# Block inverse by 32 changed columns per level, and attention steps with one wait for the scores

## The reference

```
s = einsum('bqkgd,bskd->bkgqs', q, k) * scale
p = softmax(s, axis=-1)
o = einsum('bkgqs,bskd->bqkgd', p, v)
```

```
sa = einsum('bhvk,bhk->bhv', S, kk_t)
S = S * w_t - sa * (kk_t * a_t) + v_t * k_t
y = einsum('bhvk,bhk->bhv', S, r_t)
```

## Time and profile before

| | before |
|---|---|
| median of three runs | 2634.2 us |
| the profiled execution, its own time | 2641.69 us |
| its span, first to last instruction | 2639.9 us |
| TensorE busy | 2530.2 us (96%) |
| VectorE, ScalarE, GpSimd busy | 791.9, 594.8, 234.0 us |
| mean granted TensorE clock | 0.988 |

### The profile page before, as it was taken

One profiled execution on the slowest core, in us unless ns is written; L12 is line 12 of the kernel. 1 busy time (PEld: TensorE's weight loads), 2 busy tenths in 40 slices (PEclk: granted clock), 3 DMA queues, 4 the chain that ended last, 5 costly groups with the idle time before them and its releaser, 6 DMA issues. The chain is left out here.

```text
span 2639.9 us, 51609 instructions
## 1 busy us (share of the span) xinstructions
PE 2530.2 (96%) x23368; PEld 1512.2 (57%) x23368; DVE 791.9 (30%) x1611; ACT 594.8 (23%) x1273; POOL 234.0 (9%) x243
## 2 busy tenths in 40 slices
PE   6999999999999999999999999999999999998998
PEld 4444654455555554444444446466566666687887
DVE  2542333343434422121010002441544444321101
ACT  3353332122223211020000002441332322211100
POOL 0000000122122300000000000000022222100000
PEclk9999999999999999999999999999999999999999
DMA  7102111233232334232222224112121112145553
GB/s 278 51 17 72 49 49 56 88 106 105 67 129 66 129 98 152 80 96 72 80 78 73 80 73 149 46 66 87 56 74 58 50 51 63 54 135 177 153 153 108
DMA packets 64410, 239.14 MB, mean 91 GB/s; under 512 B 7008, under 2 KB 8048, under 8 KB 63424
## 3 DMA queue, kind: packets, MB, share of 16 engines
q1 hardware_dynamic: 61824, 220.23, 26.6%
q0 software_dynamic: 2368, 15.61, 1.6%
HBM read 234.76 MB, written 1.05 MB: 89 GB/s over the span
## 5 line engine op out<-in xcount | busy, mean ns | idle before, releaser
L420 PE MATMUL psum<-normed,panel_ring 128*128 128x512 f32 (+1 forms) x3136 | 1161.2, 515 | 4.5 <-ACT normed L648 3.4
L420 PEld LDWEIGHTS psum<-normed,panel_ring 128*128 128x128 f32 x3136 | 572.6, 190 | 433.6 <-issue 384.2
L420 PE MATMUL psum<-arena 64*64 64x64 f32 (+5 forms) x15256 | 566.5, 244 | 47.1 <-DVE arena L1599 16.4
L420 PE MATMUL psum<-arena,panel_ring 128*128 128x512 f32 (+1 forms) x1792 | 606.6, 492 | 1.8 <-ACT arena L1067 1.8
L420 PEld LDWEIGHTS psum<-arena 64*64 64x64 f32 (+3 forms) x15256 | 379.3, 137 | 329.1 <-issue 215.8
L420 PEld LDWEIGHTS psum<-arena,panel_ring 128*128 128x128 f32 x1792 | 333.7, 190 | 226.3 <-issue 200.7
L714 DVE TENSOR_REDUCE softmax_stats<-psum 128x1 f32<-128x512 f32 (+1 forms) x144 | 83.9, 600 | 170.6 <-PE psum L420 169.4
L739 ACT ACTIVATE arena<-psum,softmax_stats 128x512 f32<-128x512 f32 (+1 forms) x144 | 87.8, 613 | 209.4 <-DVE softmax_stats L714 123.6
L1814 DVE TENSOR_TENSOR arena<-arena 128x512 f32<-128x512 f32 (+1 forms) x64 | 35.7, 559 | 305.1 <-ACT arena L1801 305.1
L1690 DVE SCALAR_TENSOR_TENSOR arena<-psum,modulation,arena 128x256 f32<-128x256 f32 x24 | 10.9, 481 | 313.9 <-PE psum L420 313.9
L1573 POOL TENSOR_SCALAR arena<-arena 128x64 f32<-128x64 f32 x96 | 72.3, 768 | 358.4 <-DVE arena L1612 212.0
(11 more groups left out here) (158 smaller groups left out, 1404.5 us busy)
## 6 DMA issues: line engine op xcount, KB each, us to landing
panel_ring<-panels SPq DMA_DIRECT2D x398, 512.0 KB, 3.6
arena<-panels SPq DMA_DIRECT2D x16, 512.0 KB, 14.8
arena<-small_b POOLq DMA_DIRECT2D x2, 2176.0 KB, 9.3
arena<-bias_d POOLq DMA_DIRECT2D x2, 2048.0 KB, 9.1
arena<-x_t SPq DMA_DIRECT2D x2, 1024.0 KB, 7.5
arena<-x_t POOLq DMA_DIRECT2D x1, 2048.0 KB, 14.1
arena<-const_r POOLq DMA_DIRECT2D x2, 800.0 KB, 6.6
arena<-small_c POOLq DMA_DIRECT2D x2, 768.0 KB, 4.7
```

Source lines behind the costliest of these rows:

```text
L420: return nc.tensor.matmul(out, lhsT, rhs, start=start, stop=stop, skip_group_check=check)
```

## The change

In the levels, only half the columns are computed. At level j the blocks of width w = 2^j alternate: `old` picks the blocks that are only read at this level, `new` those that change. Group T moves 32 columns of the identity (`old`), group B the 32 `new` columns of `X`, group C the 32 columns of `B`; weights stay 64x64, and the number of matmuls stays the same. Their results lie in the first half of a PSUM bank. ScalarE evacuates B with one instruction for both directions (512 elements a partition). VectorE's four instructions have 256 elements a partition, and write into `Xt` and `X` with gaps of w elements between runs of w.

In attention the first score matmul of a step waits for both exponentials of the item before, the second has no wait; and PV is issued ahead of the transposes.

```diff
+                    if exp_done.at(2 * (s - 1) + 2) > 0:
+                        e.wait_ge(exp_done.h, exp_done.at(2 * (s - 1) + 2))
                     for i in range(2):
-                        if exp_done.at(2 * (s - 1) + i + 1) > 0:
-                            e.wait_ge(exp_done.h, exp_done.at(2 * (s - 1) + i + 1))
                         mm(psum[:, i, :nk], q_of(...), k_of(t, i, nk), True, True).then_inc(scores_full.h, 1)
-                if s >= 2 and s - 2 < n_items:      # transposes of item s-2
-                    ...
                 if s >= 3 and (s - 3) % 2 == 1:     # PV
                     ...
+                if s >= 2 and s - 2 < n_items:      # transposes of item s-2, same text
+                    ...
...
-        nt, B, Xt, t2 = chunks(lw), chunks(L), chunks(e2), be
+        nt, B, Xt, t2 = chunks(lw), L, chunks(e2), be
+        half_token = lambda c: slice(c * CHUNK // 2, (c + 1) * CHUNK // 2)
+        blocks = lambda a, j, n: a.rearrange("p (b two w) -> p b two w", two=2, w=1 << j)[:, :, n, :]
+        old = lambda a, d, j: blocks(a, j, d)
+        new = lambda a, d, j: blocks(a, j, 1 - d)
...
-  p = mm(psum[half[hd], tb + d, token(c)], X[tside(d, hd), d, c, :], eye[tside(d, hd)], True, True)
+  p = mm(psum[half[hd], tb + d, half_token(c)], X[tside(d, hd), d, c, :], old(eye[tside(d, hd)], d, j), True, True)
-  p = mm(psum[half[hd], bb + d, token(c)], nt[tside(d, hd), d, c, :], X[tside(d, hd), d, c, :], True, True)
+  p = mm(psum[half[hd], bb + d, half_token(c)], nt[tside(d, hd), d, c, :], new(X[tside(d, hd), d, c, :], d, j), True, True)
-  p = mm(psum[tside(d, hd), tb + d, token(c)], Xt[half[hd], d, c, :], B[half[hd], d, c, :], True, True)
+  p = mm(psum[tside(d, hd), tb + d, half_token(c)], Xt[half[hd], d, c, :], B[half[hd], d, half_token(c)], True, True)
...
-                for d in range(2):
-                    p = nc.scalar.activation(B[:, d], chunked(psum[:, bb + d, :]), ACT.Copy)
-                p.then_inc(b_copied.h, 1)
+                nc.scalar.activation(B[:, :, :T // 2], psum[:, bb:bb + 2, :T // 2], ACT.Copy).then_inc(b_copied.h, 1)
...
-                    p = nc.vector.tensor_copy(Xt[:, d], chunked(psum[:, tb + d, :]))
+                    p = nc.vector.tensor_copy(old(Xt[:, d].rearrange("p c t -> p (c t)"), d, j),
+                                              psum[:, tb + d, :T // 2].rearrange("p (b w) -> p b w", w=1 << j))
...
-                    p = nc.vector.copy_predicated(X[:, d], wide(level(d, j), NCH), chunked(psum[:, tb + d, :]))
+                    w = 1 << j
+                    p = nc.vector.copy_predicated(
+                        X[:, d].rearrange("p c (b two w) -> p c b two w", two=2, w=w)[:, :, :, 1 - d, :],
+                        new(level(d, j), d, j).unsqueeze(1).broadcast_to([P, NCH, CHUNK // (2 * w), w]),
+                        psum[:, tb + d, :T // 2].rearrange("p (c b w) -> p c b w", c=NCH, w=w))
```

More of the change, by code:

```diff
@@ L673, in pe @@
                     t, half, nk = groups[g]
+                    if exp_done.at(2 * (s - 1) + 2) > 0:
+                        e.wait_ge(exp_done.h, exp_done.at(2 * (s - 1) + 2))
                     for i in range(2):
-                        if exp_done.at(2 * (s - 1) + i + 1) > 0:
-                            e.wait_ge(exp_done.h, exp_done.at(2 * (s - 1) + i + 1))
                         mm(psum[:, i, :nk], q_of(t, i, 2 * half + qt), k_of(t, i, nk), True, True).then_inc(scores_full.h, 1)
-                if s >= 2 and s - 2 < n_items:
[L679 to L687, removed]
                 if s >= 3 and (s - 3) % 2 == 1:
@@ L698, in pe @@
                     p.then_inc(pv_done.h, 1)
+                if s >= 2 and s - 2 < n_items:
+                    n = s - 2
+                    nk = groups[items[n][0]][2]
+                    for i in range(2):
+                        e.wait_ge(probs_ready.h, probs_ready.at(2 * n + i + 1))
+                        if probsT_ready.at(2 * (n - 1) + i + 1) > 0:
+                            e.wait_ge(probsT_ready.h, probsT_ready.at(2 * (n - 1) + i + 1))
+                        for kt in range(nk // P):
+                            p = nc.tensor.transpose(psum[:, 2 + i, kt * P:(kt + 1) * P], prob[:, n % 2, i, kt * P:(kt + 1) * P], ident)
+                        p.then_inc(probsT_full.h, 1)
                 yield
```

## The result

The kernel after takes 2621.48 us (median of 8 runs, 2614.57 to 2628.59), the kernel before beside it 2636.09 us (8 runs, 2630.48 to 2641.67). The ratio is 0.9949 with a 95% interval of 0.9931 to 0.9967. A second set, 11 runs against 20, gave 0.9959 (0.9944 to 0.9973). So the change is worth 11 to 13 us where the forecast says 22. The profiled execution took 2628.59 us, its span 2626.8 us, at a mean granted clock of 0.987 (before 0.988). It was the slowest of its eight runs; their mean clock is 0.9895.

The account below looks back on a forecast made before the run. TensorE, busy 96% of the span, was taken as the bound, so only its waits could pay; 0 - 8.1 - 12.5 - 1.4 = -22 us took the median of 2634.2 us to 2612 us, range 2596 to 2629.

Parts of the forecast that it names:

- The matmul groups: Groups T, B and C in the levels: halving moving columns saves 0 us, since the weight load sets the pace.
- Wait C: Levels: TensorE's wait ahead of group C for the copy of B shrinks with shorter evacuations, -8.1 us.
- Wait X: Levels: TensorE's wait for the masked write into X shrinks as that write gets shorter, -12.5 us.
- I take 433: Levels: a masked write of 256 elements was taken to last 433 ns whatever its runs, against 718 for 512.
- Rival (b): Levels: evacuations with gaps don't get shorter, Wait X stays, Wait C shrinks by ScalarE's part; 2625 us, chance 0.09.
- A wait gives back at most its length: Levels: caps each copy-of-B wait's gain at its idle time, counted with 0.07 us more than its row says.
- rival (d): Gain spent elsewhere: attention steps late (+6), longer X waits become VectorE backlog at the next filler; about -6, 2628 us, chance 0.08.
- Rival (c): Levels: with half the columns streaming the clock falls to 1.2 GHz more often; slower, up to 2678 us, chance 0.05.
- The clock is full in all 40 slices: Whole run before the change: the profile's clock row was read as showing full clock throughout.
- in the scan fewer records keep the full clock: Scan after the levels: 429 records in 31 us, under half a level's, keep 2.4 GHz; argued against Rival (c).
- Attention: Attention steps: PV first saves 24 switches, -2.4 us; longer waits at three places cost +1; together -1.4 us.
- waiting together loses nothing: Attention A and D: two heads' scores run side by side, so one wait is free when the second is late anyway.

Follow-up runs that it names:

- dup64: The changed kernel, but each level group moves its 32 columns twice (64 moving), only the first copy evacuated; 0.9945 of the kernel before.
- dup64_levels: dup64 with the attention steps of the kernel before; 0.9952 of the kernel before, 12.6 us faster.
- the three pairs above: Kernels with 32 against 64 moving columns, short evacuations in both, attention alike within a pair; 32 slower by 1 and 4 us, by 5 us, and faster by half a us.
- attention_only: The kernel before with only the change's attention steps, levels as before; 1.8 us faster, with an interval that holds zero.
- cols32_long: The changed kernel's 32-column groups, but evacuations as long as before and the attention of before; 1.0044 of the kernel before.
- cols64_long: cols32_long with each group moving its 32 columns twice, so 64 columns move; 1.0013 of the kernel before.

## Why the prediction came out as it did

- **The matmul groups, 0 us: right.** 1.14 and 2.07 us a burst where "1.1 to 1.16" and 2.1 were to be seen, and dup64 shows no cost for double the columns.
- **Wait C, -8.1 us: right.** 7.4 us by the sum of standstills; the row for the copy of B went from 5.9 to 0.4 us.
- **Wait X, -12.5 us: too large by 2.** 10.5 us. The step that failed is "I take 433": 16 of 80 masked writes, at level 1, took 711 to 772 ns, as long as before (pair 1.28 us). Three waits hang on a level 1; they stood at 0.56, 1.81 and 0.54 us and came to 0.52, 2.11 and 0.50. Rival (b) held there and nowhere else. The row went from 16.4 to 6.0 us, 5 forecast.
- **That what TensorE doesn't wait for is gained: mis-sized by about 6 us.** This step is in the sentence "A wait gives back at most its length", to which no loss was put. Stops inside the groups rose from 9 to 16 us; that they are stops for instruction blocks is my reading. It is the mechanism of rival (d), the gain spent elsewhere, but in a place that (d) doesn't name. With -17.9 + 6.4 = -11.5 us the levels come close to the 12.6 us that dup64_levels measured at an unchanged clock.
- **The clock, 0 us: wrong, by 0 to 5 us.** Rival (c) in a weak form. Falls like that of rows 10 happened for 27 us of the levels' time and not 7 in the profiled run, the slowest of the change; the mean clock was 0.0015 to 0.004 lower than before in the four kernels with 32 columns and short evacuations. Times 1.55 to 2.2 us per 0.001 this would be 2 to 9 us, and the three pairs above show 0 to 5. "The clock is full in all 40 slices" read the digit 9 as full: the trace of before spends 64 us at 1.2 GHz in its mean of 0.988, and has two falls in the levels, from 953.1 and from 2185.3, not one. The argument "in the scan fewer records keep the full clock" held records of other lengths, at PE busy 30.91 of 31.00 us, against those of a level, at 26.56 of 31.00, and so did not bear on a level.
- **Attention, -1.4 us: right in sum, 1.8 measured with a wide interval.** PV first gave 1.5 us in B and D of layer 0. The cost was put in the wrong place. The longer wait of 3.0 us in A did grow, to 3.8 us. But D of layer 1 refutes "waiting together loses nothing": five waits of 3.9 us in all, +1.0 us.
- **The sum.** -22 forecast; by the parts -17.9 + 6.4 - 1.8 + (0 to 5) = -13 to -8; measured -13.4 and -10.8. That the parts meet the measurement is no proof of them: two traces with the levels unchanged (before, attention_only) already differ by 4.7 us in them, so no part is known better than to 2 or 3 us.

## What to carry to other kernels

When TensorE has short, dense work with many instructions, removing its waits may give back less than they last; look at the row "issue" and at stops that recur every 127 matmuls before counting a wait as gained. Halving the moving columns behind the same 64x64 weights saved nothing on TensorE here, and with the long evacuations it lowered the clock. What gained was the shorter evacuation, and dup64 had that gain with all 64 columns moving: try both, and compare the mean clock. If two producers finish at different times, wait for each where it is needed.

## What the runs showed of the hardware that was not expected

- TensorE stops inside a group at places 127 or 128 matmuls apart, and goes on 2.2 to 2.9 us after a 16 KB packet of instructions starts; there is one packet per 126 matmuls with their loads. In the last pair's levels the places are 3.4 to 4.9 us apart. That the packet is what it waits for was not tested.
- A masked write of 256 elements takes 430 ns with runs of 4 to 32 elements in its target, 711 to 772 ns with runs of 2, and 1283 to 1524 ns where the inner loop steps 16 bytes (in target, mask and source). A plain copy with the same runs of 2 takes 408 to 426.
- With 32 moving columns in place of 64, at the same waits (cols32_long and cols64_long), the mean clock was .984 instead of .990.
- One stretch of 17.1 us at 1.2 GHz in the levels cost 0.36 us per us, not 0.5.
